# Expert rows gathered in two passes: U per slot, V per token, with one weight column per token

## The chip, the core and the metric

The kernel runs on one core of a Trainium2 chip. The metric is the device time of one execution in microseconds (us). In the traces, PE is TensorE, DVE is VectorE, ACT is ScalarE, POOL is GpSimd (here it only prepares the gathers), SP issues the plain loads and stores.

## The reference

The program is one step of a hybrid backbone with 2 layers. 640 tokens stand in 5 blocks of 128: one prompt block (n = 0 in layer 0, 5 in layer 1) and four sample blocks (n = 1 to 4, 6 to 9). Each layer mixes tokens (attention, a state-space scan, a convolution), and then sends every token through a PEER channel mixer. Only that last part is changed:

```python
idx = ...   # 8 heads x 16 best experts of 16384, for each of 128 tokens: 128 slots per token
gate = softmax(best_s)
act = gelu(einsum('thkd,td->thk', u_tab[idx], hb))     # one dot product per token and slot
return einsum('thk,thkd->td', gate * act, v_tab[idx])  # weighted sum of V rows over the slots
```

A row of `u_tab` or `v_tab` has 1024 float32 numbers, 4 KB. A block needs 128 x 128 U rows and as many V rows, 134 MB together, and ten blocks need 1342 MB. In the table `uv` in memory, each expert's U row and V row stand side by side (8 KB).

## The kernel before, in words

**Gathers.** POOL issues one indirect DMA per slot (L580): partition = token, and each token's row is the 8 KB of its expert, so one gather brings 128 x 8 KB = 1 MB, U and V together. The rows go to a ring of 5 buffers, and in the stages where the arena is free, to up to 4 more there (`SLOT_AT`, from `slot_buffers`). A buffer is used again once PE has summed its V half (`s_vs`).

**One slot.** DVE multiplies U with the token's activations and sums (`dot`, L1174), ACT takes the gelu of the 128 results (L905), DVE builds a 128x128 diagonal matrix of gate times gelu (`weigh`, L1183, four buffers `diag`), and PE multiplies the diagonal with the V half, two matmuls of 512 columns, adding to `acc` in PSUM (`add_v`, L626). In float32, each of these matmuls stands as two records in the trace. `add_peer` adds the finished block to `X` once.

**Choosing the experts.** DVE's `choose(b)` finds the 128 slots of a block from scores that PE makes in `score_block`, and `gates(b)` the gates. For sample blocks 2 to 4 these steps are set between the dots of the block before.

**Order of the work.** Each engine's program is a fixed list. The time line of a layer is: the modulation matmuls (24 units, called mod), the prompt mixer, the sample mixer, then the sample blocks' experts. The experts of the prompt block run beside the sample mixer, and those of the fourth sample block of layer 0 beside layer 1's mod and prompt mixer: a class `Beside` sets one slot (for each engine its part of it) at points of the mixer that the tables `BESIDE_SAMPLE` and `BESIDE_PROMPT` list. All other sample blocks (three in layer 0, four in layer 1) run alone.

## Time and profile before

| | us |
|---|---|
| median of 3 runs | 5156.39 (5149.72 to 5161.9) |
| the profiled execution's own time | 5157.6 |
| its span in the trace | 5155.8 |
| PE, DVE, ACT, POOL busy | 3948.3, 3243.6, 743.3, 1441.7 |
| share of the 16 DMA engines' time, gathers / plain loads | 65.1% / 9.2% |

The span is 1.8 us shorter than the execution's own time, and that time is 1.2 us above the median. Busy time says what an engine did, not what set the pace: that is read stage by stage. The stages used below begin and end at the first gather or the last matmul of a block: the start and the prompt mixer of layer 0 (to 394 us), the sample mixer (394 to 1303), three blocks alone (1303 to 2313.5), mod and prompt mixer of layer 1 beside the fourth block (to 2896), its sample mixer (to 3805), four blocks alone (to 5134), and the final norm.

### The profile page before, as it was taken

The numbers are of one execution on the slowest core, as the hardware profiler recorded it, in microseconds if no ns is written. First come the engines' busy times: TensorE is split into PE (matmuls) and PEld (weight loads), VectorE is DVE, ScalarE is ACT, GpSimd is POOL, SyncE is SP. The second block draws the span as 40 slices with busy tenths as digits, with TensorE's granted clock in tenths as the row PEclk, the third lists the DMA queues.
The fourth block names the chain that finished last, engine by engine and source line by source line (L and its number), as shares of the span: only waits on it lengthen the run. The fifth ranks groups of instructions, "written<-read, shape, count | busy, mean of one in ns | idle before, by whom it ended". The sixth has DMA issues, their size and how long they took to land. (4 is left out here: it accounts for less than half of the span.)

```text
span 5155.8 us, 36421 instructions
## 1 busy us (share of the span) xinstructions
PE 3948.3 (77%) x11046; PEld 1947.4 (38%) x11046; DVE 3243.6 (63%) x8263; ACT 743.3 (14%) x2205; POOL 1441.7 (28%) x1284
## 2 busy tenths in 40 slices
PE   5667767889777777778877885779887777787776
PEld 4545323464322222225534642445432222232222
DVE  1336576643787877864465647665368878687666
ACT  0011113510101001010012111242111010100101
POOL 0000111210444444432222011122124444344432
PEclk8778778999999999999989886889999999999999
DMA  5433345763898998998968534467559989899998
GB/s 181 144 106 118 127 165 192 254 226 129 356 414 366 421 421 365 421 418 324 353 247 321 187 131 165 171 246 252 189 209 409 419 367 421 365 421 421 415 421 344
DMA packets 342149, 1497.72 MB, mean 290 GB/s; under 512 B 31424, under 2 KB 176448, under 8 KB 178112
## 3 DMA queue, kind: packets, MB, share of 16 engines
q0 software_dynamic: 184320, 1342.26, 65.1%
q1 hardware_dynamic: 157632, 153.13, 9.2%
q8 instruction: 88, 1.44, 0.1%
q14 instruction: 109, 0.89, 0.0%
HBM read 1491.97 MB, written 3.31 MB: 290 GB/s over the span
## 5 line engine op out<-in xcount | busy, mean ns | idle before, releaser
L626 PE MATMUL expert_acc<-uv_ring,diag 128*128 128x512 f32 x3744 | 1899.9, 641 | 424.7 <-DVE diag L1183 415.9
L580 POOL DMA_INDIRECT uv_ring<-uv,expert_index x936 | 1051.6, 1124 | 2912.4 <-PE expert_acc L626 2288.2
L626 PEld LDWEIGHTS expert_acc<-uv_ring,diag 128*128 128x128 f32 x3744 | 702.6, 202 | 1518.3 <-DVE diag L1183 906.0
L1174 DVE CUSTOM_DVE_ANT_0 uv_ring<-uv_ring,arena 128x1024 f32<-128x1024 f32 x680 | 831.2, 1222 | 237.6 <-DMA uv_ring<-uv,expert_index 234.8
L626 PE MATMUL expert_acc<-arena,diag 128*128 128x512 f32 x1376 | 686.5, 631 | 258.6 <-DVE diag L1183 190.2
L1183 DVE TENSOR_SCALAR diag<-const_mats,expert_gate,gelu 128x128 f32<-128x128 f32 x1280 | 464.8, 363 | 380.6 <-ACT gelu L905 283.5
L905 ACT ACTIVATE gelu<-u_dot 128x1 f32<-128x1 f32 x1280 | 256.1, 203 | 3013.2 <-DVE u_dot L1174 3012.7
L580 POOL DMA_INDIRECT arena<-uv,expert_index x344 | 389.9, 1133 | 758.9 <-PE expert_acc L626 460.7
L1174 DVE CUSTOM_DVE_ANT_0 arena<-arena 128x1024 f32<-128x1024 f32 x344 | 420.7, 1223 | 171.6 <-DMA arena<-uv,expert_index 170.2
L626 PEld LDWEIGHTS expert_acc<-arena,diag 128*128 128x128 f32 x1376 | 245.0, 195 | 690.4 <-DVE diag L1183 408.1
L1174 DVE CUSTOM_DVE_ANT_0 uv_ring<-uv_ring,prompt_rows 128x1024 f32<-128x1024 f32 x256 | 311.5, 1218 | 80.9 <-DMA uv_ring<-uv,expert_index 80.3
L606 PE MATMUL rotating<-const_mats,arena 128*128 128x128 f32 (+1 forms) x622 | 127.3, 341 | 249.9 <-ACT arena L899 62.0
L854 PE MATMUL rotating<-hT,w_ring 128*128 128x128 f32 (+1 forms) x1024 | 286.9, 439 | 5.5 <-DMA w_ring<-w_pq 3.7
L645 PE MATMUL rotating<-w_ring,hT 128*128 128x256 f32 x768 | 210.2, 437 | 98.3 <-DMA w_ring<-w_ada 87.1
L645 PEld LDWEIGHTS rotating<-w_ring,hT 128*128 128x128 f32 x768 | 167.0, 222 | 136.5 <-DMA w_ring<-w_ada 75.2
L606 PEld LDWEIGHTS rotating<-const_mats,arena 128*128 128x128 f32 (+1 forms) x622 | 92.1, 172 | 326.0 <-ACT arena L899 67.3
L854 PEld LDWEIGHTS rotating<-hT,w_ring 128*128 128x128 f32 x1024 | 160.6, 196 | 135.1 <-issue 128.3
L681 PE MATMUL rotating<-hT,w_ring 128*128 128x512 f32 (+1 forms) x640 | 178.0, 434 | 4.2 <-DMA w_ring<-w_in 4.2
L670 PE MATMUL rotating<-w_ring,hT 128*128 128x256 f32 (+1 forms) x640 | 143.0, 388 | 33.8 <-ACT arena L938 20.4
L1538 DVE FIND_INDEX8 arena<-arena 128x8 uint32<-128x128 f32 (+1 forms) x480 | 148.9, 329 | 0.0
L827 PE MATMUL rotating<-w_ring,hT 128*128 128x256 f32 x640 | 146.0, 382 | 1.9 <-ACT hT L1064 1.9
L670 PEld LDWEIGHTS rotating<-w_ring,hT 128*128 128x128 f32 x640 | 123.9, 205 | 53.9 <-ACT arena L938 21.2
(199 smaller groups left out, 2721.8 us busy)
## 6 DMA issues: line engine op xcount, KB each, us to landing
w_ring<-w_ada SPq DMA_DIRECT2D x96, 512.0 KB
w_ring<-w_in SPq DMA_DIRECT2D x64, 512.0 KB
w_ring<-w_pq SPq DMA_DIRECT2D x64, 512.0 KB
w_ring<-w_out SPq DMA_DIRECT2D x32, 512.0 KB
uv_ring<-uv,expert_index POOLq DMA_INDIRECT x936
arena<-b_ada SPq DMA_DIRECT2D x48, 128.0 KB
arena<-uv,expert_index POOLq DMA_INDIRECT x344, 18.1
x<-x_in SPq DMA_DIRECT2D x1, 2560.0 KB, 11.7
```

What stands on the lines that cost most here:

```text
L580: pool.indirect_dma_start(out=UV[j], out_offset=None, in_=uv, in_offset=bass.IndirectOffsetOnAxis(ap=idxs[:, n % 2, k:k + 1], axis=0)).the ...
L606: return pe.transpose(out, src, C[:, C_ID, :])
L626: ins = pe.matmul(acc[:, half, :], diag[:, m % DIAGS, :], UV[SLOT_AT[m]][:, D + 512 * half:D + 512 * half + 512], start=(k == 0), stop=(k ...
L645: ins = pe.matmul(t[:, 0:WU], hT[:, c, 0:P], w[:, c, :], start=(c == 0), stop=(c == DC - 1))
L670: ins = pe.matmul(t[:, 0:width], hT[:, c, b * P:(b + 1) * P], w[:, c, 0:width], start=(c == 0), stop=(c == DC - 1))
L681: ins = pe.matmul(t[:, 0:T], w[:, c, k * P:(k + 1) * P], hT[:, c, 0:T], start=(c == 0), stop=(c == DC - 1))
L827: ins = pe.matmul(t[:, 0:WU], hT[:, c, b * P:(b + 1) * P], w[:, c, :], start=(c == 0), stop=(c == DC - 1))
L854: ins = pe.matmul(t[:, 0:T], w[:, c, k * P:(k + 1) * P], hT[:, c, 0:T], start=(c == 0), stop=(c == DC - 1))
L905: nc.scalar.activation(gel[:, m % DOTS:m % DOTS + 1], dots[:, m % DOTS:m % DOTS + 1], ACT.Gelu).then_inc(s_gel, 1)
L1174: V_.tensor_tensor_reduce(UV[j][:, 0:D], UV[j][:, 0:D], rows_of(n), 1.0, 0.0, ALU.mult, ALU.add, dots[:, m % DOTS:m % DOTS + 1]).then_inc( ...
L1183: V_.tensor_scalar(diag[:, m % DIAGS, :], C[:, C_ID, :], gat[:, n % 2, k:k + 1], gel[:, m % DOTS:m % DOTS + 1], ALU.mult, ALU.mult).then_i ...
L1538: ins = V_.max_index(dst[:, r, at_], val[:, r, at_], src(r))
```

## The change

U and V are gathered apart, as rows of 4 KB from the same table seen as half rows (the index is doubled, V's has 1 added). A U gather has one slot of all 128 tokens, as before. A V gather has all 128 slots of **one token**: partition = slot. Its indices are a column of the block's index matrix turned by PE (`turn_index`, drained with +1 by ACT). For V, PE then needs no diagonal: for each token one column of 128 weights (gate times gelu, turned by `turn_weights`) is multiplied with the token's 128 rows. The column stands among 31 zero columns of `wcol`, so that the product lands in the token's row of a group of 32 output rows. A round takes four tokens, one from each group of 32, with 8 matmuls (4 groups x 2 halves, 128 rows x 32 columns, 512 columns streamed); 32 rounds make a block. All weights of a block must be there first, so V runs one block later than U: gelu is one ACT instruction per block, `weigh` one DVE multiply per block.

The buffers are twice as many and half as big (10 in the ring, up to 8 in the arena). Beside the sample mixer, the prompt block's slots begin with the first stage of the mixer and stand closer, and its rounds follow; the fourth sample block of layer 0 now has its U part alone and only its V rounds beside mod and the first part of the prompt mixer. A rotating PSUM bank is given to the turned matrices (6 to 5 banks). In the core of the diff, function by function:

```diff
-RING, SPARE = 5, 4
-DIAGS, DOTS = 4, 16
+RING, SPARE = 10, 8
+QUAD = P // 4
+ROUNDS = P // 4
+CHUNK = 4
+V_STEP = SLOTS + 5
+LEAD = 12
-BESIDE_SAMPLE = points(("n1", [7], 2), ("pa", range(4), 2), ("pa", range(4, 8), 1), ("px", range(6), 1),
-                       ("pg", range(4), 1), ("conv", [5], 4), ("taps", range(4, 30, 5), 2), ("cT", [3], 4), ("st", range(8), 3), ("yT", [3], 3), ("v", [4], 3), 
-                       ("head", range(0, 24, 2), 2), ("head", range(1, 24, 2), 1), ("wo", range(16), 1), ("n2", [7], 3), ("pq", range(8), 2))
+BESIDE_SAMPLE = points(("n1", [7], 2), ("pa", range(8), 4), ("pz", range(8), 4), ("px", range(6), 3),
+                       ("pg", range(4), 3), ("conv", [5], 8), ("taps", range(4, 30, 5), 4), ("cT", [3], 6), ("st", range(8), 3), ("yT", [3], 3), ("v", [4], 3),
+                       ("head", range(24), 1))
+BESIDE_PROMPT = points(("mod", range(24), 1), ("n1", [1], 1), ("pa", range(2), 1), ("pz", range(2), 1), ("px", range(6), 1),
+                       ("pg", range(4), 1))
...
+def gather_order():
+    for l in range(L):
+        n = l * NBLK
+        for k in range(SLOTS):
+            yield "u", n, k
+        for m in range(ROUNDS):
+            yield "v", n, m
+        for b in range(4):
+            n = l * NBLK + 1 + b
+            lead = SLOTS if b == 0 else LEAD
+            for k in range(lead):
+                yield "u", n, k
+            for m in range(ROUNDS if b else 0):
+                yield "v", n - 1, m
+                for k in range(lead + 4 * m, min(lead + 4 * m + 4, SLOTS)):
+                    yield "u", n, k
+        for m in range(ROUNDS):
+            yield "v", l * NBLK + 4, m
...
 def _(pool):
+                for q in range(1 if kind == "u" else 4):
+                    j, turn, before = U_AT[(n, i)] if kind == "u" else V_AT[(n, i, q)]
...
+                    buffer_free(before)
+                    ix = idxs[:, n % 2, i:i + 1] if kind == "u" else idxT[:, QUAD * q + i:QUAD * q + i + 1]
+                    pool.indirect_dma_start(out=rows_at[j], out_offset=None, in_=half_rows,
+                                            in_offset=bass.IndirectOffsetOnAxis(ap=ix, axis=0)).then_inc(s_gat[j], 16)
...
-            def add_v(n, k):
-                pe.wait_ge(s_dg, m + 1)
-                for half in range(2):
-                    ins = pe.matmul(acc[:, half, :], diag[:, m % DIAGS, :], UV[SLOT_AT[m]][:, D + 512 * half:D + 512 * half + 512],
+            def add_round(n, m):
+                for q in range(4):
+                    pe.wait_ge(s_gat[V_AT[(n, m, q)][0]], 16 * V_AT[(n, m, q)][1])
+                for half in range(2):
+                    for q in range(4):
+                        mid = WCOLS * (1 + part * 4 * CHUNK + q * CHUNK + m % CHUNK)
+                        ins = pe.matmul(acc[QUAD * q:QUAD * q + QUAD, half, :], wcol[:, mid - m:mid - m + WCOLS],
+                                        rows_at[V_AT[(n, m, q)][0]][:, 512 * half:512 * half + 512],
...
+            def weights_of(n):
+                act.wait_ge(s_dot, (n + 1) * SLOTS)
+                nc.scalar.activation(dots[:, n % 2], dots[:, n % 2], ACT.Gelu).then_inc(s_gel, 1)
+            def drain_index(n):
+                act.wait_ge(s_ixp, n + 1)
+                if n:
+                    act.wait_ge(s_vs, n * ROUNDS)
+                nc.scalar.activation(idxT[:], turned[:, 1, :], ACT.Copy, bias=1.0).then_inc(s_ixT, 1)
...
-            def weigh(n, k):
-                V_.tensor_scalar(diag[:, m % DIAGS, :], C[:, C_ID, :], gat[:, n % 2, k:k + 1], gel[:, m % DOTS:m % DOTS + 1],
+            def weigh(n):
+                V_.tensor_tensor(w, w, dots[:, n % 2], ALU.mult).then_inc(s_wt, 1)
```

The orders of POOL, PE and DVE while sample blocks run alone, before and after. Names: `uv_ring`, `row_ring` and `arena` are row buffers, `expert_index` the index matrix, `index_turned` the turned one; in brackets stand the waits.

POOL, in the middle of a block, before, and then the change:

```order
L580 DMA uv_ring<-uv,expert_index 128x2048 [waits v_summed] x5
L580 DMA arena<-uv,expert_index 128x2048 [waits v_summed] x2
L580 DMA uv_ring<-uv,expert_index 128x2048 [waits v_summed] x5
L580 DMA arena<-uv,expert_index 128x2048 [waits v_summed] x2
L580 DMA uv_ring<-uv,expert_index 128x2048 [waits v_summed] x5
```

```order
L640 DMA row_ring<-uv,index_turned 128x1024 [waits v_summed] x2
L640 DMA arena<-uv,index_turned 128x1024 [waits v_summed] x2
L640 DMA row_ring<-uv,expert_index 128x1024 [waits u_dotted] x4
L640 DMA row_ring<-uv,index_turned 128x1024 [waits v_summed]
L640 DMA arena<-uv,index_turned 128x1024 [waits v_summed] x3
L640 DMA arena<-uv,expert_index 128x1024 [waits u_dotted]
```

POOL's list had one gather of 1 MB per slot; now four V gathers and four U gathers of half the size take turns, and a block has 256.

PE at the same place, two slots before, and one round of the change:

```order
L626 MATMUL expert_acc<-arena,diag 128x512 [waits diag_ready]
L626 MATMUL expert_acc<-arena,diag 128x512
L626 MATMUL expert_acc<-uv_ring,diag 128x512 [waits diag_ready]
L626 MATMUL expert_acc<-uv_ring,diag 128x512
L626 MATMUL expert_acc<-uv_ring,diag 128x512 [waits diag_ready]
```

```order
L706 MATMUL expert_acc<-row_ring,weight_columns 32x512 [waits rows_gathered10,rows_gathered11,rows_gathered6,rows_gathered7,weight_columns_ready,peer_added]
L706 MATMUL expert_acc<-arena,weight_columns 32x512 x2
L706 MATMUL expert_acc<-row_ring,weight_columns 32x512 x2
L706 MATMUL expert_acc<-arena,weight_columns 32x512 x2
L706 MATMUL expert_acc<-row_ring,weight_columns 32x512
L706 MATMUL expert_acc<-arena,weight_columns 32x512 [waits rows_gathered2,rows_gathered3,rows_gathered9,rows_gathered13]
```

The number of matmuls stays: 8 for four slots before, 8 for four tokens now; each now fills 32 rows of the output, and PE waits for the gathers themselves and no longer for a DVE result per slot.

DVE at the beginning of a sample block, before and after:

```order
L1174 ISA arena,u_dot<-arena 128x1024 [waits rows_gathered5,ht_drained,gates_ready]
L1174 ISA u_dot 128x1
L1531 MAX arena<-arena 128x8 [waits ps_drained]
L1531 MAX arena<-arena 128x8 x3
L1183 TENSOR_SCALAR diag<-const_mats,expert_gate,gelu 128x128 [waits gelu_done,v_summed]
L1174 ISA arena,u_dot<-arena 128x1024 [waits rows_gathered6]
```

```order
L1318 ISA arena,u_dot<-arena 128x1024 [waits rows_gathered11,weights_ready,ht_drained]
L1318 ISA u_dot 128x1
L1318 ISA row_ring,u_dot<-row_ring,arena 128x1024 [waits rows_gathered7]
L1318 ISA u_dot 128x1
L1325 TENSOR_TENSOR expert_gate<-expert_gate,u_dot 128x128 [waits gelu_done]
L1318 ISA row_ring,u_dot<-row_ring,arena 128x1024 [waits rows_gathered0]
L1318 ISA u_dot 128x1
```

The 128 diagonal products of a block are gone from DVE, and one product of the whole weight matrix of the block before stands behind the second dot.

## Rows read from the trace of the kernel before

**Rows 1.** The page, section 2: what the DMA engines moved in 40 slices, GB/s

```profile
GB/s 181 144 106 118 127 165 192 254 226 129 356 414 366 421 421 365 421 418 324 353 247 321 187 131 165 171 246 252 189 209 409 419 367 421 365 421 421 415 421 344
```

**Rows 2.** Windows: stretch and length; busy us by engine (instructions), TensorE clock, DMA share, GB/s

```profile
185.00:393.00 208.00, 125.38 (x717) 104.31 (x717) 82.48 (x284) 32.36 (x93) 0.00 (x0) 0.75 0.35 109
466.00:1303.30 837.30, 678.69 (x2022) 364.15 (x2022) 464.22 (x1169) 186.82 (x427) 138.88 (x128) 0.88 0.50 180
1303.30:1637.70 334.40, 256.27 (x514) 92.70 (x515) 276.41 (x726) 34.66 (x141) 155.70 (x128) 0.95 0.98 402
1643.00:1975.50 332.50, 250.31 (x514) 90.86 (x515) 254.23 (x616) 28.93 (x132) 145.94 (x128) 0.96 0.98 404
2313.50:2537.00 223.50, 180.81 (x594) 113.98 (x594) 90.18 (x205) 10.50 (x47) 53.18 (x44) 0.93 0.91 340
2537.00:2896.10 359.10, 286.19 (x1053) 165.81 (x1052) 201.33 (x531) 66.86 (x191) 80.43 (x79) 0.89 0.82 300
3805.20:4140.10 334.90, 252.42 (x514) 89.36 (x515) 275.95 (x726) 34.67 (x141) 155.18 (x128) 0.97 0.97 401
4812.40:5134.30 321.90, 253.78 (x513) 88.68 (x512) 204.89 (x386) 25.74 (x127) 120.72 (x120) 0.98 0.98 406
```

The five busy times of a row are, in this order, those of PE, PE's weight loads, DVE, ACT and POOL.

**Rows 3.** The page, section 4: the chain that ended last, by engine

```profile
DMA 12%; DVE 3%; PE 3%; issue 1%; ACT 0%; POOL 0%; DVEq 0%; POOLq 0%
```

**Rows 4.** Timeline of POOL and PE in the last block: start, length, idle before and releaser

```profile
5041.70 1.00 POOL L580 DMA_INDIRECT uv_ring<-uv,expert_index  x1 [1.50 <-PE expert_acc L626]
5044.19 0.98 POOL L580 DMA_INDIRECT uv_ring<-uv,expert_index  x1 [1.49 <-PE expert_acc L626]
...
5041.93 1.98 PE L626 MATMUL expert_acc<-uv_ring,diag 128*128 128x512 f32 x4 [0.51 <-DVE diag L1183]
```

**Rows 5.** Timeline of POOL at its first gathers, nothing to wait for

```profile
468.04 0.94 POOL L580 DMA_INDIRECT uv_ring<-uv,expert_index  x1 [0.30 <-issue]
469.28 0.94 POOL L580 DMA_INDIRECT uv_ring<-uv,expert_index  x1 [0.31 <-issue]
```

**Rows 6.** Timeline of POOL and PE between two sample blocks

```profile
1620.00 0.98 POOL L580 DMA_INDIRECT arena<-uv,expert_index  x1 [1.50 <-PE expert_acc L626]
1642.96 0.94 POOL L580 DMA_INDIRECT arena<-uv,expert_index  x1 [21.97 <-PE rotating L845]
...
1638.44 3.74 PE L845 MATMUL rotating<-keys_s,arena 128*128 128x128 f32 x32
```

**Rows 7.** Timeline: gathers on POOL and dots on DVE in the same microseconds

```profile
2018.65 0.94 POOL L580 DMA_INDIRECT arena<-uv,expert_index  x1 [0.30 <-issue]
2021.38 1.86 POOL L580 DMA_INDIRECT uv_ring<-uv,expert_index  x1 [0.54 <-PE expert_acc L626]
...
2018.71 1.23 DVE L1174 CUSTOM_DVE_ANT_0 uv_ring<-uv_ring,arena 128x1024 f32<-128x1024 f32 x1 [0.32 <-DMA uv_ring<-uv,expert_index]
2021.20 1.23 DVE L1174 CUSTOM_DVE_ANT_0 uv_ring<-uv_ring,arena 128x1024 f32<-128x1024 f32 x1 [0.22 <-DMA uv_ring<-uv,expert_index]
```

**Rows 8.** Groups of DVE in the block 1643 to 1975.5: count, busy us, mean ns, idle before

```profile
L1183 DVE TENSOR_SCALAR diag<-const_mats,expert_gate,gelu 128x128 f32<-128x128 f32 x128 | 46.6, 364 | 31.6 <-ACT gelu L905 18.2 <-PE expert_acc L626 12.3
L1558 DVE TENSOR_TENSOR arena<-const_mats,arena 128x1024 f32<-128x1024 f32 x4 | 4.9, 1222 | 0.1
```

**Rows 9.** The same groups in the block 1303.3 to 1637.7

```profile
L1183 DVE TENSOR_SCALAR diag<-const_mats,expert_gate,gelu 128x128 f32<-128x128 f32 x128 | 48.4, 378 | 27.2 <-ACT gelu L905 22.9 <-PE expert_acc L626 2.7
```

**Rows 10.** The chain in order of time, two pieces: V matmuls back to back; a landing

```profile
4497.54 20.96 PE expert_acc L626 x44
...
4520.69 19.02 DMA uv_ring<-uv,expert_index
```

**Rows 11.** Groups of ACT in layer 1's prompt mixer, 2537 to 2896

```profile
L905 ACT ACTIVATE gelu<-u_dot 128x1 f32<-128x1 f32 x82 | 16.5, 202 | 159.2 <-DVE u_dot L1174 159.1
L905 ACT ACT_TABLE_LOAD x7 | 9.0, 1283 | 0.1
```

**Rows 12.** The page, section 3: DMA queues, packets, MB, share of 16 engines

```profile
q0 software_dynamic: 184320, 1342.26, 65.1%
q1 hardware_dynamic: 157632, 153.13, 9.2%
```

More of the change, by code:

```diff
@@ L134 @@
 SECOND_AT, GATES_AT = 30, 122
-def slot_buffers():
-    place, before, turn = [], [], []
-    used, times = {}, {}
-    for n in range(L * NBLK):
-        b = n % NBLK - 1
-        alone = b >= 0 and (b < 3 or n // NBLK == L - 1)
-        ring = range(RING + (min(b + 2, SPARE) if alone else 0))
-        for k in range(SLOTS):
-            j = min(ring, key=lambda x: used.get(x, -1))
-            place.append(j)
-            before.append(used.get(j, -1))
-            turn.append(times.get(j, 0) + 1)
-            used[j], times[j] = n * SLOTS + k, turn[-1]
-    return place, before, turn
@@ L564, in _ @@
         def _(pool):
[L565 to L581 removed]
+            pool.memset(wcol[:], 0.0).then_inc(s_zero, 1)
@@ L914, in _ @@
+            beside = Beside(weigh_beside)
+            act.wait_ge(s_const.sem, 16 * 8)
             act.wait_ge(s_x.sem, 16)
```

326 lines of the change are left out of this document (209 added, 117 removed).

## The prediction

> **What bounds the kernel now.** The page comes first: its line of GB/s [rows 1] shows two kinds of stretches. Where sample blocks run alone it stands at 421 GB/s and dips to 350 to 365 between blocks; beside a mixer it is at 125 to 250. The chain that ended last [rows 3] covers only the last 1034 us, four blocks alone, and its largest part is the landing of gathers. The windows by stage [rows 2] say the same: in a block alone the DMA engines are 98% busy, while DVE has 254 to 276 of some 333 us, PE 250 and POOL 146 to 156. The timeline of the last block [rows 4] gives the beat, one gather of 1 MB every 2.49 us, with POOL idle for 1.50 us of it: POOL waits for a buffer that PE gives back, and the buffer was late because its rows landed late (a landing takes 19.02 us from issue [rows 10], eight other gathers are ahead of it). So alone the kernel is bound by transfer. Between blocks POOL stands still from 1620.00 to 1642.96 [rows 6], since the next block's spare buffers wait for PE's scores, which are behind the last V matmul; some 20 us are lost there, four times in all. Beside a mixer nothing is full, and the fixed order of the engines sets the pace: every slot costs time there. The two prompt mixers price it: 208.0 us in layer 0 without a slot, 359.1 in layer 1 with 82 [rows 2, 11], so 151/82 = 1.84 us per slot.
>
> **The gather queue, the term that decides.** The change moves the same bytes with twice the gathers: 256 per block instead of 128. What one costs POOL is read where nothing holds it up: 0.94 us and 0.30 of issue, one every 1.24 us [rows 5]. 1 MB then takes 2.48 us of POOL, all of the 2.49 us beat, and its 1.50 us of slack is spent. It gets worse where a dot runs. Two neighbours in the trace [rows 7]: a gather that begins 0.06 us before a dot takes 0.94 us; one that begins 0.18 us after a dot's start, with 1.05 us of the dot left, takes 1.86 us, that is 0.94 and what was left of the dot less 0.13. The dot keeps its 1.23 us in both. So a gather that starts within a dot waits for its end. If the two engines' starts are independent, a gather inside a dot loses (1.22 - 0.13)^2 / (2 x 1.22) = 0.49 us in the mean. The operations with this effect take 128 x 1.22 = 156 us of a block, and ten of `choose` with two operands in SBUF, 1.22 us each as the group of four [rows 8], 12 more: 168. The time T of a block with both U and V gathers is 256 x 1.24 + 256 x (168/T) x 0.49, which gives **T = 374 us**. The ends are 328 us (no gather is ever held: transfer is the bound, 256 gathers of at least 524288 B / 421 GB/s = 1.245 us, with 1.28 taken because smaller packets carry less per engine second: 8 KB rows 65.1% for 1342 MB, the plain loads of mostly 1 KB 9.2% for 153 MB, 24% more for a byte [rows 12], of which I give a tenth) and 443 us (every gather held for 0.49). I take the middle one: dots fill 45% of 374 us, and the spread of starts in the trace is wide.
>
> **Part by part**, against the execution's 5157.6 us.
>
> *Start and prompt mixer of layer 0, to 394 us:* POOL clears `wcol` long before its first gathers at 468 us [rows 5]; nothing changes.
>
> *Three blocks alone, layer 0, 1303.3 to 2313.5, 1010 us.* Now block 1's U part alone, then three stretches with V of one block and U of the next. The U part is bound by DVE: 276.4 us in that block less the 48.4 of `weigh` [rows 2, 9] is 228; I add 22 for waits that stay and for the handover to V (last dot, gelu, index drained, first V landing), 250 us. The halts of 20 us between blocks go: `score_block` now stands ahead of the rounds, and 12 U gathers (`LEAD`) cover the turning of the next indices. 250 + 3 x 374 = 1372, **+362**. Both DVE's 46.6 us of `weigh` per block [rows 8] and its waits for gelu leave a queue that no longer sets the pace and are worth nothing here.
>
> *Mod and prompt mixer of layer 1, 2313.5 to 2896.1, 582.6 us.* The U rows of the fourth block are gone from here (they are in the third stretch above). Mod had two slots of 1 MB per unit and now has one round of 2 MB: same bytes, 340 GB/s at a DMA share of 0.91 [rows 2], so I keep its 223.5 us. The prompt mixer is that of layer 0, 208, plus the last 8 rounds at 3 us: 24. Sum 455.5, **-127**.
>
> *Two sample mixers, 394 to 1303.3 and 2896.1 to 3805.2, 909 us each.* Before: 128 slots x 1.84 = 235 us of path. Now 128 dots at 1.22 on DVE (156) and 32 rounds on PE. A round is 16 records; 44 of them back to back take 20.96 us [rows 10], 0.476 each, so 7.6 us if they run one after another, 1.9 if the four column groups run at once. No row shows matmuls of this shape. I take 1.9, though the nearest row is the serial one, because the four write disjoint quarters of the output rows with separate weights, and nothing orders them; the other end is a rival below. Rounds: 61 us. Half of these lie beside softmax work in the attention heads (-30), and ACT reloads its table less often (7 loads of 1.28 us for 82 slots [rows 11], with as many back, -20). 156 + 61 - 50 = 167, against 235 that is -68; the first stages are crowded, since the choice of experts and 52 dots now fall into 16 short steps, and I give 8 back: **-60 each, -120**. The Trainium skill ("TensorE: Matmul & The Clock Gate", Part 3: Packing small matmuls) lets each column group run on its own and gives 2.38x for three groups; no run here shows it, and with that factor in place of 4 a round would be 3.2 us and the sum 40 us higher. The clock stood at 0.95 to 0.98 in the blocks alone [rows 2]; if it falls with PE's load, a round gets longer where PE has slack to spare.
>
> *Four blocks alone, layer 1, 3805.2 to 5134.3, 1329 us.* 250 + 3 x 374, then the last block's V rows without dots: 128 x 1.28 = 164, and 18 around them (the turned index must wait for the last round of the block before, about 10 us without a gather; 8 for the last landing and round). 1554, **+225**.
>
> The final norm stays. Sum: 362 - 127 - 120 + 225 = +340, so 5157.6 + 340 = **5498 us**, 6.6% above the execution and as much above the median, which is 1.2 us lower. What is late next everywhere alone is the next gather's descriptors; PE (7.6 us of an 11.7 us round at most) and DVE (254 - 47 = 207 of 374) wait.
>
> **The rivals.**
> *A. The gathers are not held, transfer stays the bound.* For it: POOL's 1.24 us fits under 1.28 us, and dots that follow landings at a steady beat may always start in the same place. Against it: that margin is 0.04 us and the hold is plain. T = 328: six stretches save 46 each, 5498 - 276 = 5222.
> *B. Column groups do not run at once*, so that the change only renames PE's work. A round costs 7.6. Alone it hides under 11.7 us, but mod, where PE is busy 180.8 us with 44 slots of 1.9 us among them [rows 2], so 4.0 us per unit of its own, becomes 11.6 against 9.3 us per unit, +56; 8 rounds of the prompt mixer +37; the last V part 243 against 164, +79; two mixers with half of 32 x 5.7 on the path, +182. 5498 + 354 = 5852.
> *C. Every gather is held*, because dots and gathers lock into a beat in which each waits. T = 443 at the end, 410 halfway: six times +36 to +69, 5714 to 5912.
> *D. Faster.* One mechanism: the mixers lose more than I give, since a slot's chain DVE, ACT, DVE, PE is cut from them. Place: 394 to 1303 and 2896 to 3805. Even with A's transfer bound (5222), each mixer must lose 60 + 33 = 93 us to break even; with T = 374 it is 230, all that 128 slots cost now. At 150 each with A: 5042. Against it: the dots alone cost 156.
>
> **How the numbers follow.** The forecast 0.54, A 0.15, B 0.11, C 0.11, D 0.09. The range 5200 to 5830 takes in the forecast with its own spread (5400 to 5620), A, and most of C, and leaves out D, B and C's far end, together 0.2. Something over 0.2% (10 us) can be told from no change here: faster 0.09, same 0.02, slower 0.89.
>
> **What would show it.** Right: in the blocks alone POOL's busy share rises from 45% to over 90% with gaps of 0.30 us put down to "issue", the mean gather is 1.1 to 1.3 us there, GB/s falls from 421 to about 360, and DMA share to 0.85. Two stretches of 250 us, six of 374 without halts. Round matmuls of about 2 us. Wrong: 421 GB/s alone (A), a PE busy over 7 us per round (B), gathers of mean 1.5 us (C), a sample mixer under 820 us (D). The sum would be wrong at its root if POOL still waited for `v_summed` or `u_dotted` in the stretches with U and V.

## The result, and the profile after

The changed kernel takes 5588.06 us in the median of 4 runs (5567.17 to 5605.79), the kernel before 5159.15 us (5149.72 to 5166.48): a ratio of 1.0831, 95% interval 1.0785 to 1.0877. The forecast was 5498 us, slower; the time is 90 us above it and inside the range. The profiled execution took 5567.17 us, its span is 5565.1 us.

Four lines of the page answer to [rows 1], [rows 3] and [rows 12]: the TensorE clock in 40 slices with what the DMA engines moved, the chain that ended last, and the gather queue.

```profile
PEclk8777668896556555656886785787955556555567
...
GB/s 183 117 114 253 215 112 315 155 58 244 293 355 366 356 362 371 358 369 345 294 327 123 104 355 144 187 328 39 120 280 300 361 370 356 364 361 360 374 353 324
...
q0 software_dynamic: 368640, 1342.34, 65.2%
...
POOL 32%; PE 21%; DVE 19%; issue 14%; DMA 9%; another core or an unknown queue 3%; ACT 2%; SPq 1%; DVEq 0%; POOLq 0%; ACTq 0%
```

The same bytes pass in twice the packets (368640 for 184320), and the plateau of 421 GB/s has become one of 345 to 374. POOL heads the chain, with "issue" (the 0.30 us between its gathers). The windows by stage, with the columns of [rows 2]:

```profile
393.00:1249.30 856.30, 538.67 (x2150) 313.61 (x2150) 498.02 (x1291) 108.99 (x273) 286.72 (x256) 0.78 0.51 181
1249.30:1501.20 251.90, 33.95 (x118) 18.47 (x116) 220.12 (x580) 9.21 (x19) 162.62 (x127) 0.57 0.77 262
1501.20:1877.80 376.60, 115.12 (x521) 27.57 (x521) 222.89 (x515) 9.73 (x24) 282.89 (x257) 0.58 0.95 355
1877.80:2250.60 372.80, 119.08 (x554) 27.87 (x554) 212.80 (x491) 9.53 (x23) 278.66 (x257) 0.58 0.96 363
2250.60:2628.50 377.90, 120.12 (x547) 23.65 (x547) 161.01 (x263) 6.13 (x18) 261.25 (x257) 0.61 0.94 360
2628.50:2868.80 240.30, 147.51 (x709) 97.28 (x713) 23.89 (x68) 2.56 (x9) 76.86 (x82) 0.82 0.84 301
2868.80:3127.20 258.40, 160.48 (x941) 112.94 (x941) 85.46 (x288) 33.84 (x95) 43.22 (x46) 0.77 0.52 184
3127.20:3980.30 853.10, 539.91 (x2149) 315.40 (x2150) 499.11 (x1291) 109.09 (x274) 293.93 (x256) 0.78 0.51 181
4234.50:4609.50 375.00, 113.66 (x521) 27.50 (x521) 220.62 (x511) 9.73 (x24) 282.64 (x256) 0.58 0.96 355
5356.50:5543.60 187.10, 107.02 (x513) 23.17 (x512) 2.06 (x3) 1.99 (x9) 119.91 (x128) 0.76 0.95 359
```

From the top: the sample mixer of layer 0; a block's U part alone; three stretches with U of one block and V of the block before it; modulation; prompt mixer of layer 1; its sample mixer; a stretch of layer 1; the last V part. In a stretch DVE has at most 223 us of 375 and PE about 120, so neither sets the pace. POOL does. Its 257 gathers from 1877.80 to 2250.60 take 278.66 us where 257 x 0.94 is 241.6: 37 us of holds. The 0.30 us between them are 77. That makes 356; the other 17 us are halts that have another cause, below. The third stretch of a layer is made up differently: its holds come to 20 us (261.25 less 241.6), and its halts to 26. The first line below is a part of POOL's groups from 1877.80 to 2250.60, the others are its waits with an unnamed releaser ("remote") from 2250 to 2628 and over the whole kernel (us in total, times, longest):

```profile
L640 POOL DMA_INDIRECT row_ring<-uv,index_turned x69 | 76.3, 1106 | 34.7 <-issue 19.2 <-remote 13.6 <-PE expert_acc L706 1.8
...
POOL row_ring L640 <- remote: 26.1, 8, 4.8
...
POOL row_ring L640 <- remote: 160.3, 61, 4.8
```

The timeline of POOL and DVE in that stretch shows the holds of [rows 7] again:

```profile
2001.77 1.66 POOL L640 DMA_INDIRECT row_ring<-uv,expert_index  x1 [0.30 <-issue]
...
2003.73 0.94 POOL L640 DMA_INDIRECT row_ring<-uv,index_turned  x1 [0.30 <-issue]
...
2006.55 1.21 DVE L1318 CUSTOM_DVE_ANT_0 row_ring<-row_ring,arena 128x1024 f32<-128x1024 f32 x1
...
2006.69 1.89 POOL L640 DMA_INDIRECT arena<-uv,index_turned  x1 [0.30 <-issue]
```

The gather at 2006.69 began 0.14 us into a dot and took 1.89 us; it ended 0.82 us after the dot. That is the rule in the whole trace: of the 369 gathers that start 0.1 us or more into a dot with at least 0.3 us of it left, each one is held and ends 0.81 to 0.82 us after the dot. The 755 dots that start well within a gather keep their 1.20 to 1.23 us. PE's rounds are the last thing the forecast had no row for. Two of them, each 16 records, the second in eight pairs (the first and the last are shown):

```profile
2683.90 1.92 PE L706 MATMUL expert_acc<-row_ring,weight_columns 128*32 128x512 f32 x16
...
2003.17 1.07 PE L706 MATMUL expert_acc<-row_ring,weight_columns 128*32 128x512 f32 x2 [8.52 <-DMA arena<-uv,index_turned]
...
2005.75 1.07 PE L706 MATMUL expert_acc<-arena,weight_columns 128*32 128x512 f32 x2
```

The four column groups run at once: 1.92 us a round at the 2.4 GHz level. In the stretches the granted clock is 0.57 to 0.61 where it was 0.95 to 0.98 [rows 2], mostly at the 1.2 GHz level, and a round takes 3.65 us there. PE waits 8.52 us before it, so that costs next to nothing.

### The profile page after: what moved, and what is told of

Same layout as the page of the kernel before. It is cut to its first block, busy times and chain, and to the rows that moved or that the text cites. A ratio compares the mean times of both kernels' runs of the same rounds, so it can differ in the third digit from the quotient of the medians.

```text
span 5565.1 us, 34833 instructions
## 1 busy us (share of the span) xinstructions
PE 2511.1 (45%) x11066; PEld 1256.4 (23%) x11066; DVE 2858.8 (51%) x7011; ACT 363.8 (7%) x932; POOL 2800.3 (50%) x2565
## 3 DMA queue, kind: packets, MB, share of 16 engines
q0 software_dynamic: 368640, 1342.34, 65.2%
## 4 chain that ended last, share of the span: by engine, by line
POOL 32%; PE 21%; DVE 19%; issue 14%; DMA 9%; another core or an unknown queue 3%; ACT 2%; SPq 1%; DVEq 0%; POOLq 0%; ACTq 0%
POOL row_ring L640 21%; POOL arena L640 11%; PE rotating L939 5%; DVE row_ring L1318 5%; DMA w_ring<-w_ada 4%; PE expert_acc L706 4%; DMA row_ring<-uv,index_turned 4%; PE rotating L912 3%; PE rotating L730 2%; DVE arena L1473 2%; DVE arena L1678 1%; PE rotating L666 1%; DVE arena L1671 1%; PE rotating L827 1%
## 5 line engine op out<-in xcount | busy, mean ns | idle before, releaser
L640 POOL DMA_INDIRECT row_ring<-uv,expert_index x968 | 1111.1, 1148 | 1728.7 <-DVE expert_index L1746 1154.0
L706 PE MATMUL expert_acc<-row_ring,weight_columns 128*32 128x512 f32 x3596 | 992.7, 874 | 1133.5 <-DMA arena<-uv,index_turned 511.4
L640 POOL DMA_INDIRECT row_ring<-uv,index_turned x899 | 928.1, 1032 | 772.4 <-PE expert_acc L706 290.7
L1318 DVE CUSTOM_DVE_ANT_0 row_ring<-row_ring,arena 128x1024 f32<-128x1024 f32 x712 | 859.5, 1225 | 677.5 <-DMA row_ring<-uv,expert_index 604.4
L706 PE MATMUL expert_acc<-arena,weight_columns 128*32 128x512 f32 x1524 | 691.4, 1003 | 525.7 <-DMA row_ring<-uv,index_turned 418.4
L706 PEld LDWEIGHTS expert_acc<-row_ring,weight_columns 128*32 128x32 f32 x3596 | 184.7, 139 | 1669.8 <-issue 1669.1
L640 POOL DMA_INDIRECT arena<-uv,index_turned x381 | 425.2, 1116 | 124.7 <-issue 113.2
L1318 DVE CUSTOM_DVE_ANT_0 row_ring<-row_ring,prompt_rows 128x1024 f32<-128x1024 f32 x256 | 304.2, 1224 | 42.0 <-DMA row_ring<-uv,expert_index 34.3
L730 PE MATMUL rotating<-w_ring,hT 128*128 128x256 f32 x768 | 222.4, 455 | 163.4 <-DMA w_ring<-w_ada 156.2
L1671 DVE MAX8 arena<-arena 128x8 f32<-128x128 f32 (+1 forms) x480 | 123.8, 328 | 142.2 <-ACT arena L1216 131.6
```

Source lines behind the costliest of these rows:

```text
L640: pool.indirect_dma_start(out=rows_at[j], out_offset=None, in_=half_rows, in_offset=bass.IndirectOffsetOnAxis(ap=ix, axis=0)).then_inc(s_g ...
L706: ins = pe.matmul(acc[QUAD * q:QUAD * q + QUAD, half, :], wcol[:, mid - m:mid - m + WCOLS], rows_at[V_AT[(n, m, q)][0]][:, 512 * half:512 ...
L730: ins = pe.matmul(t[:, 0:WU], hT[:, c, 0:P], w[:, c, :], start=(c == 0), stop=(c == DC - 1))
L1318: V_.tensor_tensor_reduce(rows_at[j], rows_at[j], rows_of(n), 1.0, 0.0, ALU.mult, ALU.add, dots[:, n % 2, k:k + 1]).then_inc(s_dot, 1)
L1671: ins = V_.max(dst[:, r, at_], src(r))
```

## The experiments

The question is what made a stretch 374 us: the number of gathers, what the dots hold, the bytes, or the order. Times in brackets are the lowest and highest of a kernel's runs. The four kernels that follow ran on one chip (no run of the changed kernel itself is on record for it). In the code, "..." marks what is left out.

**Half the V bytes, all the gathers.**

```diff
+            quarter_rows = uv.rearrange("n (s d) -> (n s) d", s=4)
-                    pool.indirect_dma_start(out=rows_at[j], out_offset=None, in_=half_rows,
...
+                    u = kind == "u"
+                    pool.indirect_dma_start(out=rows_at[j] if u else rows_at[j][:, 0:D // 2], out_offset=None, in_=half_rows if u else quarter_rows,
...
-                nc.scalar.activation(idxT[:], turned[:, 1, :], ACT.Copy, bias=1.0).then_inc(s_ixT, 1)
+                nc.scalar.activation(idxT[:], turned[:, 1, :], ACT.Copy, bias=2.0, scale=2.0).then_inc(s_ixT, 1)
```

> The changed kernel, but a V gather fetches a quarter row (2 KB for each token) where it fetched a half row (4 KB). The sums over V still read whole 4 KB rows, so that half of what they add is stale: half of the V bytes is left out, and no instruction is. The count of gathers stays, and so does each dot. Theory A (the U+V stretches are set by POOL's own time on 257 gathers, 1.24 us each, plus holds by the dots): the stretches stay at 370 to 378 us; the V-only tails, in which POOL waited (1.405 us a gather), fall from 187 to about 128 x 1.24 = 159 plus 5, 23 us less each; the stage of modulation and prompt mixer of layer 1 falls from 500 us towards the predicted 456 if its surplus of 44 us is the V transfers beside the weight loads. Sum about 5588 - 2 x 23 - 0 to 44 = 5500 to 5540 us. Theory B (they are set by the transfers: 256 x 1.40 = 359 of 374 us): three quarters of the bytes take 269 us, so POOL's 319 to 330 us rule, six stretches fall by some 45 us each, and the time is about 5230 to 5270 us.

Measured: 5381.84 us (5380.73 to 5382.96), 1.0415 of the kernel before (1.0339 to 1.049). Windows of a stretch, of modulation and prompt mixer in two pieces, and of the last V part:

```profile
4087.60:4455.20 367.60, 116.89 (x533) 28.23 (x537) 223.34 (x513) 9.73 (x24) 289.60 (x256) 0.57 0.82 276
2576.60:2847.00 270.40, 209.12 (x1135) 132.88 (x1136) 36.49 (x115) 7.64 (x24) 121.35 (x128) 0.88 0.79 263
2847.00:3016.80 169.80, 95.34 (x513) 76.46 (x511) 72.97 (x242) 28.80 (x80) 0.00 (x0) 0.71 0.28 88
5191.40:5357.40 166.00, 93.30 (x513) 19.60 (x512) 2.04 (x3) 1.98 (x9) 121.05 (x128) 0.73 0.68 203
```

A quarter of the bytes of a stretch is gone (276 GB/s, DMA share 0.82), and it still takes 368 us: theory B falls. POOL is busy for 289.60 us in it, 49 us above 256 x 0.94, so the holds even grew. What did react is modulation with prompt mixer, 440 us for 499, and the two sample mixers (751.6 us from the first U gather to the next block's, for 782.4; 744.8 for 779.2 in layer 1). The changed kernel's times are not from the same chip, as far as is recorded; the kernel with 24 extra gathers, below, had all its bytes on this one. Its mixers took 772.1 and 768.8 us, so 20 and 24 us are what the bytes surely cost there, and its stretches 344 to 361, so here the stretches gained nothing at all from fewer bytes. The whole came out 120 us below theory A's lower end: I had not thought of the mixers as short of transfers.

**No second operand in the dot.**

```diff
-                V_.tensor_tensor_reduce(rows_at[j], rows_at[j], rows_of(n), 1.0, 0.0, ALU.mult, ALU.add,
-                                        dots[:, n % 2, k:k + 1]).then_inc(s_dot, 1)
+                V_.tensor_reduce(dots[:, n % 2, k:k + 1], rows_at[j], AX.X, ALU.add).then_inc(s_dot, 1)
```

> The changed kernel, but the dot of a U slot (a product of two tiles in SBUF, summed) is a plain sum of the gathered row: the multiplication by the token is left out, one tile is read and nothing is written over the row. Gathers and bytes are the same. Theory A (POOL's 1.24 us a gather plus holds by the dots make 374 us): the holds go, no gather takes over 1.0 us for a dot's sake, and a U+V stretch comes down to the next bound, the transfers' 256 x 1.40 = 359 us; POOL then waits now and then. Six stretches less by 10 to 15 us each and the two blocks of U alone unchanged: 5588 - 60 to 90 = 5500 to 5530 us. Theory B (the holds are no more than the time that a transfer-bound POOL would have waited anyway): 374 us stays within 3 us, and the time within 20 us of the changed kernel's. Theory C (transfers leave room): a stretch falls to 257 x 1.24 = 319 us, six times 55 less, about 5260 us.

Measured: 5264.72 us (5260.87 to 5268.57), 1.0188 of the kernel before (1.0112 to 1.0264). Two stretches:

```profile
1475.40:1805.70 330.30, 109.12 (x505) 26.40 (x505) 222.57 (x378) 9.73 (x24) 244.15 (x257) 0.55 1.01 400
1805.70:2136.30 330.60, 119.40 (x554) 26.37 (x554) 210.55 (x363) 9.30 (x23) 246.61 (x256) 0.59 1.03 409
```

None of the three sums: a stretch falls by 44 us, to 330 (the third of a layer to 346), and the DMA engines are full at 409 GB/s, so the transfers' floor is 256 x 524288 B / 409 GB/s = 328 us, the prediction's 1.28 us a gather. The 1.40 us that I read from the changed kernel's last V part was no floor. The halts are gone too. The sum keeps DVE as long as the dot did, so time on DVE is not what the hold comes from. (Theory C's 5260 us was hit, but by 319 us and a wrong floor; only how the terms lie decides here.) One piece of the timeline has both kinds side by side; it is from the repetition of this kernel on another chip, the last experiment:

```profile
1900.23 1.22 DVE L1318 TENSOR_REDUCE u_dot<-row_ring 128x1 f32<-128x1024 f32 x1 [2.07 <-DMA row_ring<-uv,expert_index]
...
1900.51 0.94 POOL L640 DMA_INDIRECT row_ring<-uv,expert_index  x1 [0.30 <-issue]
...
1901.37 1.22 DVE L1701 TENSOR_TENSOR arena<-arena 128x1024 f32<-128x1024 f32 x1
...
1901.75 1.64 POOL L640 DMA_INDIRECT arena<-uv,expert_index  x1 [0.30 <-DVE u_dot L1318]
```

The gather that starts within the sum of one tile takes 0.94 us; the one that starts 0.38 us into an operation on two tiles takes 1.64 and ends 0.80 us after it. In this kernel all 680 gathers that start well inside a sum take 0.93 to 0.95 us. The edit takes away two things at once, though: the second tile that is read, and the tile that is written. It doesn't tell which of them holds, and the first trace has no simple answer: a gather that starts within a copy of one 128x512 tile to another (at 2484.60 us) takes 1.19 us and ends 0.81 us after it, one within a MATCH_REPLACE8, which also reads one tile and writes one (at 1551.97 us), takes 0.94. The Trainium skill ("SBUF — State Buffer", SBUF: two separate sides) has a vector operation with two SBUF inputs lock a port pair against a GpSimd operation that reads SBUF, for its whole length; by that rule the trace agrees, 0.94 and 1.64 us.

**Both edits.** The two diffs above together.

> Both edits at once in the changed kernel: V gathers of 2 KB for each token (half of the V bytes is left out) and a plain sum of the U row in place of the dot (the multiplication is left out). If gathers cost POOL 0.94 + 0.30 = 1.24 us whatever they carry, and dots and bytes are all else that counts, a U+V stretch is 257 x 1.24 = 319 us, with POOL never waiting: six stretches less by 55 us each, two tails less by 23, the stage of modulation and prompt mixer less by 0 to 44: 5588 - 330 - 46 - 22 = about 5190 us, range 5150 to 5230. If DVE's sum or TensorE's rounds of the V groups at the 1.2 GHz level bound instead, it stays above 340 us with POOL waiting for one of them, and the time above 5320 us.

Measured: 5110.09 us (5100.54 to 5119.64), 0.9889 of the kernel before (0.9805 to 0.9973). A stretch of layer 0:

```profile
1790.30:2114.60 324.30, 119.46 (x550) 29.01 (x554) 211.13 (x363) 9.53 (x23) 246.26 (x256) 0.57 0.90 313
```

324 us with the DMA engines no longer full. 256 x 1.24 = 317 and 6 us of holds by the operations that choose experts (246.26 less 240.6) make it. The time is 40 us below the range given, because the mixers shortened too (745 and 738 us from the first U gather to the next block's), which that sum leaves out. So POOL's bare count of gathers alone takes nearly the 333 us that a block took before.

**What a gather costs POOL.** 24 extra gathers at the start, while VectorE and ScalarE wait ("..." stands for the semaphores and the clearing of the index tile):

```diff
...
+            table = uv.rearrange("n (s d) -> (n s) d", s=2)
+            done = 0
+            for parts in (128, 64, 32, 128):
+                for r in range(6):
+                    pool.indirect_dma_start(out=rows_ring[0:parts, r, :], out_offset=None, in_=table,
+                                            in_offset=bass.IndirectOffsetOnAxis(ap=idxT[0:parts, r:r + 1], axis=0)).then_inc(s_mic, 16)
+                    done += 16
+                pool.wait_ge(s_mic, done)
...
```

> The changed kernel with 24 extra gathers at its start, on an otherwise idle chip: six each with 128, 64, 32 and 128 partitions, 4 KB each, all from row 0. Nothing is left out; ScalarE and VectorE start after them. If POOL's 0.94 us is a price per gather, all four sixes show 0.94 us. If it is a price per row that is addressed, they show 0.94, about 0.5, about 0.25 and 0.94 us (6 to 7 ns a row); between the two, a fixed part and a part per row can be read off. The whole kernel comes out 20 to 60 us later than the changed kernel. A price per gather leaves it possible to save POOL time by larger gathers; a price per row does not, and says that the change doubled POOL's work because it doubled the rows.

Measured: 5457.07 us, in a single execution. One gather of each size, 64, 32 and 128 rows:

```profile
23.34 0.90 POOL L622 DMA_INDIRECT row_ring<-uv,index_turned  x1 [0.30 <-issue]
...
38.91 0.86 POOL L622 DMA_INDIRECT row_ring<-uv,index_turned  x1 [0.30 <-issue]
...
47.83 0.94 POOL L622 DMA_INDIRECT row_ring<-uv,index_turned  x1 [0.30 <-issue]
```

The price is one per gather: 0.94 us for 128 rows, 0.86 for 32, so about 0.83 us and less than a nanosecond a row, and the 0.30 between. Neither the rows' number (by more than 0.08 us) nor, by [rows 5] against the changed kernel, their length (8 KB or 4 KB) matters. But the whole time was a surprise: 24 more gathers, and 110 us less than the lowest run of the changed kernel. I followed that up below.

**The split alone.** From here on each time is the median of four executions. This kernel and the next three shared a chip. In the kernel before, each 8 KB gather becomes two of 4 KB, with nothing else changed:

```diff
-                            pool.indirect_dma_start(out=UV[j], out_offset=None, in_=uv,
-                                                    in_offset=bass.IndirectOffsetOnAxis(ap=idxs[:, n % 2, k:k + 1], axis=0)).then_inc(s_gat[j], 16)
+                            for h in range(2):
+                                pool.indirect_dma_start(out=UV[j][:, D * h:D * h + D], out_offset=None, in_=uv, element_offset=D * h,
+                                                        in_offset=bass.IndirectOffsetOnAxis(ap=idxs[:, n % 2, k:k + 1], axis=0)).then_inc((s_gat, s_gatv)[h][j], 16)
...
+                pe.wait_ge(s_gatv[SLOT_AT[m]], SLOT_TURN[m] * 16)
```

> The kernel before, but each slot's gather of an 8 KB row is two gathers of 4 KB, U half and V half, each with a semaphore of its own. Dots, weigh operations, matmuls, order and bytes stay. Theory A (POOL's price per gather and the dots' holds set the U+V stretches): 257 x 1.24 = 319 us plus 20 to 42 us of holds and the halt of 20 us between blocks; a block alone goes from 333 to 365 to 385 us, seven of them, and the blocks beside sample mixer and prompt stage hide it: 5159 + 7 x 32 to 52 = about 5385 to 5520 us, most likely 5450. Then nearly the whole loss of the change is in the doubled gathers. Theory B (gathers cost only with the order and the turning of the change): 333 us stays, 5150 to 5180 us.

Measured: 5533.9 us (5513.86 to 5540.75), 1.0714 of the kernel before (1.0683 to 1.0745). Two blocks alone, of layer 0 and of layer 1:

```profile
1694.20:2081.60 387.40, 263.24 (x552) 98.42 (x552) 262.97 (x616) 32.39 (x138) 287.88 (x257) 0.93 0.93 347
4762.10:5138.40 376.30, 263.23 (x500) 93.55 (x501) 263.04 (x611) 28.51 (x130) 296.64 (x257) 0.92 0.96 354
```

Theory A: +376 us of the change's +429, without V by tokens, without one block's delay. Its size is 14 us above the upper end (+51 us per block alone: the seven together took 2697 us for 2339), and POOL is busy 46 to 55 us above its bare count. The halts with an unnamed releaser are here as well, 51 us of them, so they don't belong to V by tokens:

```profile
POOL uv_ring L582 <- remote: 32.0, 14, 4.4
...
POOL arena L582 <- remote: 19.0, 7, 4.1
```

The changed kernel on the same chip took 5593.05 us: all else in the change adds 59 us in sum.

**The scores earlier, in the kernel before.**

```diff
-                        if b + 1 < nb:
-                            score_block(b + 1)
+                        if b == 0:
+                            score_block(1)
...
                             add_v(n, k)
+                            if k == SCORES_AT and b + 2 < nb:
+                                score_block(b + 2)
```

> The kernel before, but the scores of block b+2 are computed by TensorE within block b's slots (behind slot 64), where before block b+1's scores came ahead of block b's first slot. Nothing is left out. Theory A (the halt of some 20 us between two blocks is the chain scores, top choices, gates, which then begins half a block earlier): four to five halts of 20 us fall to a few us, about 5060 to 5090 us, below both kernels. Theory B (the halt is POOL's wait for ring slots or for the last weigh operations): the time stays within 10 us of 5159 us.

Measured: 5111.71 us (5101.52 to 5123.54), 0.9908 of the kernel before (0.9878 to 0.9937): faster than both kernels, by a small amount that is clear of the noise. POOL at the place of [rows 6], and a block:

```profile
1623.68 0.98 POOL L581 DMA_INDIRECT arena<-uv,expert_index  x1 [1.50 <-PE expert_acc L627]
1624.97 1.49 POOL L581 DMA_INDIRECT arena<-uv,expert_index  x1 [0.30 <-issue]
```

```profile
1625.00:1948.90 323.90, 252.68 (x550) 94.59 (x549) 253.65 (x614) 31.52 (x137) 152.75 (x128) 0.97 1.01 417
```

The halt of 22 us is gone, as theory A had it, but the gain is 46 us and not the 70 to 100 it gave: from first gather to first gather, a block that took 338 us (1643.0 to 1980.8) takes 324, since 128 x 1.049 MB at 417 GB/s are 322. In the kernel before, the transfers caught up on a part of each halt; now they are the whole of it.

**The V rounds all beside the modulation, in the changed kernel.**

```diff
-BESIDE_PROMPT = points(("mod", range(24), 1), ("n1", [1], 1), ("pa", range(2), 1), ("pz", range(2), 1), ("px", range(6), 1),
-                       ("pg", range(4), 1))
+BESIDE_PROMPT = points(("mod", range(8), 1), ("mod", range(8, 24), 2))
```

> The changed kernel, but the 32 rounds of V of layer 0's last block all lie beside the modulation (one each beside its first eight units, two beside the next, up to the 32nd), and none beside the prompt mixer's steps. Same instructions. I predicted 455.5 us for modulation and prompt mixer of layer 1 and the first profile showed 500 (234 and 258). Theory A (V gathers and weight loads share the transfers; what matters is that 67 MB of V rows and the weights must pass in these 500 us, and each round costs TensorE 3.4 us at the 1.2 GHz level): the prompt mixer falls to about 210 us and the modulation grows to 265 to 285; the sum is 480 to 500 us, and the kernel within 25 us of the changed kernel. Theory B (the surplus is waits that the prompt mixer's short chain suffers for each V round): the sum falls to 455 us or below, and the kernel by 40 us or more.

Measured: 5572.54 us (5566.24 to 5581.69), 1.0808 of the kernel before (1.0781 to 1.0835); the changed kernel beside it took 5593.05. Modulation, prompt mixer:

```profile
2634.90:2911.60 276.70, 182.63 (x918) 102.61 (x914) 24.84 (x69) 3.29 (x12) 120.45 (x128) 0.81 0.94 348
2911.60:3127.10 215.50, 129.96 (x737) 108.73 (x733) 85.35 (x288) 33.60 (x93) 0.00 (x0) 0.74 0.35 109
```

As theory A had it: 216 and 277 us, together 492 for 499. The prompt mixer is within 8 us of its 208 of [rows 2], and the modulation has nearly what it lost. Beside the half V bytes (440 us), this says that V rows and weights share the transfers there. PE's waits for weights in modulation, in the changed kernel and then in the kernel before (us in total, times, longest):

```profile
PE rotating L730 <- DMA w_ring<-w_ada: 86.1, 13, 11.3
...
PE rotating L645 <- DMA w_ring<-w_ada: 16.9, 8, 6.0
```

**The changed kernel again, and the halts.** No edit.

> The changed kernel once more, beside others on one chip. In its first profile POOL stood still ahead of some V quadruples for 2 to 4.8 us with a releaser that the trace can't name (10 such halts, 24.6 us, in the last tail alone, where a gather took 1.405 us); with 24 extra gathers at the start none of them was left, the tail's gathers came every 1.24 us, and the kernel took 5457 us where it had taken 5567 to 5606. Theory A: the halts belong to the run (how the 16 DMA engines fall out of step when the transfers are at their limit), so a repetition may fall anywhere from 5440 to 5610 us, and a profile under 5500 us shows stretches of 350 to 362 us without the halts. Theory B: the extra gathers at the start removed them, and the unchanged code takes 5560 to 5610 us again with the halts in it.

Measured: 5593.05 us (5581.15 to 5602.94), 1.0834 of the kernel before (1.0807 to 1.0861). The time is theory B's, and the halts are there again. POOL's waits in the last V part, 5356 to 5544, first profile of the changed kernel (us in total, times, longest):

```profile
POOL row_ring L640 <- remote: 24.6, 10, 4.2
...
POOL arena L640 <- ACT index_turned L1008: 8.8, 1, 8.8
POOL row_ring L640 <- PE expert_acc L706: 0.3, 1, 0.3
```

And the same part, 5260 to 5434, of the kernel with 24 extra gathers, its first time:

```profile
POOL arena L653 <- ACT index_turned L1021: 11.5, 1, 11.5
POOL row_ring L653 <- PE expert_acc L719: 1.8, 6, 0.3
```

Beside the one wait for the turned index nothing there stands still for longer than 0.3 us, and the part takes 173.5 us for 187.1. What the DMA engines do in a halt and in the 4 us after it, in the changed kernel:

```profile
5423.30:5427.40 4.10, 3.34 (x9) 0.64 (x10) 0.00 (x0) 0.00 (x0) 0.01 (x1) 0.52 1.03 412
5427.40:5431.40 4.00, 4.00 (x27) 1.18 (x19) 0.00 (x0) 0.00 (x0) 3.04 (x4) 0.64 0.76 228
```

They are full while POOL stands, and run short afterwards. Did the extra gathers do that? Three kernels on a further chip: the same code again, 24 extra gathers that all have 128 rows (`for parts in (128, 128, 128, 128)`), and one extra gather of 64 rows (`for parts in (64,)`, `range(1)`).

> The changed kernel with 24 extra gathers at its start (six each with 128, 64, 32 and 128 rows), a second time. Theory A (the extra gathers take away the halts of 2 to 4.8 us that stand before V quadruples in both profiles of the changed kernel): 5440 to 5480 us again. Theory B (that one look was a lucky run): 5580 to 5630 us, with the halts back and a tail whose gathers come every 1.41 us.

> The changed kernel with 24 extra gathers at its start, all of them with 128 rows, 4 KB each, from row 0; nothing left out. They cost some 45 us at the start, part of it hidden. Theory A1 (what removed the halts is where the gathers' descriptors lie in the queue, and only gathers with fewer rows than 128 shift that pattern): the halts stay, and the kernel takes 5590 to 5640 us. Theory A2 (any extra gathers, or the writes to index tile and ring, do it): no halts, 5440 to 5480 us.

> The changed kernel with a single extra gather at its start, with 64 rows. It costs some 10 us at the start, most of it hidden behind the constants' loads. Theory A1 (the lie of the descriptors in the queue makes the halts): one short gather shifts all later ones, the halts go, and the kernel takes 5420 to 5460 us, 130 to 170 less than the changed kernel. Theory A2 (it takes many extra gathers, or a late start of ScalarE and VectorE): the halts stay and it takes 5580 to 5620 us.

Measured: 5627.74 us (5614.29 to 5631.47), 5638.56 (5628.22 to 5646.73) and 5589.42 (5578.97 to 5596.11), or 1.0915 (1.0887 to 1.0942), 1.0944 (1.0915 to 1.0973) and 1.0848 (1.082 to 1.0876) of the kernel before. All three have the halts; one stretch of each took 372 us, where the first execution of the 24 gathers' code took 354. Theory B for the first: the extra gathers remove nothing, they cost some 40 us (38 and 49 more than a single one). With that both theories of the other two have lost their ground; the one short gather removed no halt, as its theory A2 had it, and the 24 full ones neither. So one execution of this code took 170 us less than the median of four others on another chip, while the kernel before differed by 0.3% between the two.

**The sum again**, on a fourth chip (no new edit):

> The changed kernel with a plain sum of the U row in place of the dot (the multiplication by the token is left out), a second time. The four kernels that I ran first, on one chip, showed no halt of POOL ahead of V quadruples; all profiles of the changed kernel and of its variants on other chips show them, and the same code with 24 extra gathers took 5457 us there and 5628 us elsewhere. So the 5265 us of this edit must be compared within its own chip: 5457 less some 40 us for the extra gathers is 5415, and the holds are worth 150 us, 25 us in each of six stretches. Theory A (the halts are the chip's): on a chip with halts this edit takes 5400 to 5450 us, its tail's gathers come every 1.40 us, and a stretch takes 350 to 360 us; on a chip without them it takes 5255 to 5275 us. Theory B (the halts need the holds, so that a kernel without holds has none on any chip): 5255 to 5275 us here too, with the kernel before at 5150 to 5165 us.

Measured: 5270.03 us (5265.97 to 5272.81), 1.0209 of the kernel before (1.0188 to 1.0231). No halts, gathers of the last V part 1.24 us apart, stretches of 326 to 332 us. That is the value theory B gave, or theory A for a chip without halts; which of the two this chip is, no run shows.

## Why the prediction was right, and where it was off

**Direction and mechanism.** POOL's 1.24 us per gather takes the place of the transfer as the bound: right. The bare count (324 us with 6 of holds, of 374), the split alone (+376 of +429 us) and the insensitivity to bytes (368 us with a quarter less) show it, each apart.

**T = 374.** Measured 370 to 378 in six stretches, but not from the terms that I had: that the number fits is luck. I gave 56 us to holds on top of 317. By the three rows above, holds are 37 to 42 us in a layer's first two stretches and 16 to 17 us are halts with no releaser in the trace; in the third stretch holds are 20 and 28 us, and halts 26 and 23. Over the six, holds come to 206 us for the 338 forecast, and 115 us are halts, of which the forecast had none. The step that failed is "if the two engines' starts are independent": that gives about 100 held gathers in 256, and in the timeline 64 to 68 take over 1.0 us in the first two stretches, 42 and 51 in the third. What a held gather loses was about right: 0.47 to 0.64 us in the mean, for 0.49, or 0.55 without the starts in a dot's last 0.13 us. The holds also differ between kernels in stretches with as many dots, from 32 us (the extra gathers' second execution, 273.87 less 241.6) to 55 (the split kernel's block at 4762). The sum was right by two errors that nearly cancel.

One of the signs could not have come true: POOL's busy share was to rise over 90%, but 0.30 us of idle time between any two gathers leaves at most 79% of 374 us by the forecast's own terms. It is 75% (278.66 of 372.8 us).

**Rival A's floor of 1.28 us** is real (409 GB/s, 330 us a stretch), and the first two stretches of the kernel without holds sit on it. It wasn't the case here because of the holds and the halts. My forecast of the DMA share, 0.85, was low: 0.94 to 0.97. By the bytes alone it would be 328/374 = 0.88; the rest is not explained.

**U parts alone, 250:** 251.9. **Blocks of layer 0, 1372:** 1379. **Layer 1, 1554:** 1563, with 187 for the last V part for my 182.

**Mod and prompt mixer, 455.5:** 499, the one term that was mis-sized by much, 43 of the 69 us between 5498 and the profiled execution. I counted 24 rounds beside mod and 8 beside the prompt mixer; the timeline has 19 and 13, because the list's first five steps of this stage hold no round yet. The 13 took the prompt mixer from 208 to 258.4 us, 3.9 us each, where I had 8 at 3 us. Mod, with five rounds fewer than I counted, took 240.3 us for 223.5. Until its first round POOL issues only ten gathers and then waits, and the DMA engines are not full:

```profile
2628.50:2683.90 55.40, 29.99 (x105) 24.06 (x105) 5.45 (x17) 0.62 (x3) 9.42 (x10) 0.78 0.74 244
...
2686.13 0.94 POOL L640 DMA_INDIRECT row_ring<-uv,index_turned  x1 [45.46 <-PE expert_acc L706]
```

The V rows are then squeezed into the rest of the stage, where they meet the weights (13 waits, 86.1 us), and the prompt mixer waits for V rows too (13.0 us in 5 waits). Shown is that the bytes cause the surplus (440 us with half of them, 492 with the rounds elsewhere); that the late first round makes it worse is only read.

**Sample mixers, 849:** 856 and 853. Rounds at 1.9 us at the high clock: right, so rival B falls. Half the V bytes took 31 and 34 us from them (20 and 24 within one chip), which no term of mine contained.

**Rival C** falls (gathers have a mean of 1.08 us in a stretch, 278.66 over 257). **Rival D** fails in its place: the mixers lost 53 and 56 us, not 230.

## What to carry to other kernels

Before a transfer is split into smaller gathers, count gathers and not bytes: each costs POOL 1.24 us here, of 4 KB rows or 8, and 1.16 us even with 32 rows for 128, and where the old beat was 2.49 us per 1 MB, that was all the room there was. Count next what DVE does meanwhile, since a gather that starts inside an operation such as the dot, which reads two tiles and writes one, waits for its end, and one inside a sum of a single tile doesn't. And look at a halt in an otherwise full queue first: moving a block of scores by half a block gave 0.9%, where the regrouping cost 8%.

## What was not expected of the hardware

- The halts. In six of seven profiles of the changed kernel's order with its dots and full rows, POOL stands still for 2 to 5 us at a time, 128 to 161 us in all, with the releaser called "remote"; in the last V part always before the third gather of a round and mostly every 20 gathers (in the first profile at 5423.31, 5452.0, 5480.6 and 5509.4). They weren't there in the one execution of 5457 us, and their sum is about what that one took less. They weren't there without the dots' second operand either, on two chips, nor with half the V bytes, which ran only on the chip of the 5457 us. The split kernel has them (51 us), the kernel before has none. What releases them, and whether they belong to a chip, stays open: no run of the changed kernel as it is is on record for that chip.
- Less data, longer stretches: on that one chip, a stretch with full V rows took 344 to 361 us, one with half of them 366 to 372, with POOL busy 275.56 and 289.60 us in two of them. When the transfers push back a little, gathers and dots seem to fall into a beat with fewer holds; that is argued from these numbers, not shown.
- PE's granted clock fell from 0.96 to 0.58 in stretches where its busy share fell from 75% (250.31 of 332.5 us) to 32%, and a round of 16 records went from 1.92 to 3.65 us. In the stretches it cost next to nothing, since PE waited 8.52 us for the next round's rows.
